# Attention: the output weights split inside the first two tiles, the keys' copy ahead of the sinks, the sinks read as one row

## The reference

```
q = rope(hn @ w_q) * HEAD_DIM**-0.5                    # 16 heads of 64
s = where(band, q @ k.T, -inf)                         # 128 queries x 256 keys of a block
m = max(max(s), sink)                                  # one sink per head
e = exp(s - m)
pr = e / (sum(e) + exp(sink - m))
o = pr @ v                                             # (seq, 1024)
h = h + o @ w_o                                        # w_o is 1024 x 1024
```

## Time and profile before

| | us |
|---|---|
| median of 3 runs | 5109.37 |
| lowest and highest | 5103.85, 5109.4 |
| the profiled execution | 5106.4 |
| its span, first to last instruction | 5104.7 |

### The profile page before, as it was taken

The page is one execution under the profiler, slowest core; times in us unless marked ns, Lnnn a source line. Parts: engine busy times, 40 slices in busy tenths (PEclk is TensorE's granted clock), DMA queues, the critical chain, the costliest instruction groups (busy, mean ns, idle before and its releaser), DMA issues. The chain is left out here.

```text
span 5104.7 us, 90848 instructions
## 1 busy us (share of the span) xinstructions
PE 4660.7 (91%) x29444; PEld 2961.6 (58%) x29509; DVE 2867.1 (56%) x5891; ACT 2022.9 (40%) x2962; POOL 1585.7 (31%) x1163
## 2 busy tenths in 40 slices
PE   7985999999995999999589999986999999997999
PEld 6953677676663444444256666643676667665444
DVE  5774444444444555555378888873445444443676
ACT  5844443343332222222145555534343343331443
POOL 1103443444340111111033333312444444431332
PEclk9987999999997999999799999997999999999999
DMA  7968999998996666666367677757999989985664
GB/s 232 323 225 299 297 323 305 289 322 283 292 287 189 184 186 187 187 185 182 88 160 177 175 179 179 177 179 260 297 314 311 296 295 318 284 275 172 246 233 169
DMA packets 1217386, 1220.13 MB, mean 239 GB/s; under 512 B 880656, under 2 KB 908304, under 8 KB 1217296
## 3 DMA queue, kind: packets, MB, share of 16 engines
q1 hardware_dynamic: 1171216, 1051.21, 68.2%
q0 software_dynamic: 46080, 167.79, 9.4%
HBM read 738.57 MB, written 270.53 MB: 198 GB/s over the span
## 5 line engine op out<-in xcount | busy, mean ns | idle before, releaser
L824 POOL TENSOR_TENSOR ex_w_lo<-ex_raw,ex_w_hi 128x2048 bf16<-128x2048 f32 x192 | 780.4, 4093 | 1154.6 <-ACT ex_w_hi L882 1154.6
L882 ACT ACTIVATE ex_w_hi<-ex_raw 128x2048 bf16<-128x2048 f32 x384 | 707.2, 1900 | 395.4 <-PE ex_ps_y L110 190.7
L986 PE MATMUL ex_ps_gate<-ex_xT,ex_w_hi 128*128 128x0 bf16 x2048 | 569.4, 278 | 160.4 <-DMA ex_xT<-ex_xrow 132.3
L987 PE MATMUL ex_ps_gate<-ex_xT,ex_w_hi 128*128 128x0 bf16 x2048 | 569.2, 278 | 0.0
L988 PE MATMUL ex_ps_gate<-ex_xT,ex_w_lo 128*128 128x0 bf16 x2048 | 568.7, 278 | 0.0
L986 PE MATMUL ex_ps_up<-ex_xT,ex_w_hi 128*128 128x0 bf16 x2048 | 558.4, 273 | 0.0
L987 PE MATMUL ex_ps_up<-ex_xT,ex_w_hi 128*128 128x0 bf16 x2048 | 558.3, 273 | 0.0
L988 PE MATMUL ex_ps_up<-ex_xT,ex_w_lo 128*128 128x0 bf16 x2048 | 558.3, 273 | 0.0
L966 DVE COPY ex_y<-ex_ps_y 128x512 f32 x324 | 224.1, 692 | 567.0 <-PE ex_ps_y L110 522.8
L950 DVE TENSOR_TENSOR ex_aT<-ex_silu,ex_ps_up 128x384 bf16<-128x384 f32 x256 | 141.8, 554 | 708.6 <-PE ex_ps_up L988 525.2
L108 PE MATMUL ex_ps_y<-ex_w_hi,ex_aT 128*128 128x512 bf16 x1296 | 493.0, 380 | 8.1 <-DVE ex_aT L954 7.6
(11 more groups left out here) (345 smaller groups left out, 9693.2 us busy)
## 6 DMA issues: line engine op xcount, KB each, us to landing
ex_raw<-in_w_exp_gate SPq DMA_DIRECT2D x128, 1024.0 KB, 10.9
ex_raw<-in_w_exp_up SPq DMA_DIRECT2D x128, 1024.0 KB, 12.5
ex_raw<-in_w_exp_down SPq DMA_DIRECT2D x128, 1024.0 KB, 7.2
y_rows<-ex_y SPq DMA_DIRECT2D x162, 512.0 KB
up_rows<-rt_up_out SPq DMA_DIRECT2D x64, 512.0 KB, 2.6
cb_hin<-h_mid SPq DMA_DIRECT2D x64, 512.0 KB, 3.5
cb_up_in<-up_rows SPq DMA_DIRECT2D x64, 512.0 KB
mix_x<-in_x SPq DMA_DIRECT2D x32, 512.0 KB, 5.3
```

Source lines behind the costliest of these rows:

```text
L824: eng.tensor_tensor(w_lo[u][:, w], raw[:, c, :], w_hi[u][:, w], ALU.subtract).then_inc(lo_done, 1)
L882: act.activation(w_hi[u][:, c * WCHUNK:(c + 1) * WCHUNK], raw[:, c, :], ACT.Copy).then_inc(hi_done, 1)
L986: pe.matmul(out, hi, x_hi, start=j == 0, stop=False)
L987: pe.matmul(out, hi, x_lo, start=False, stop=False)
```

## The change

The block `split_weights` is gone. Four buffers `raw` belong to attention now, and the split is done among the pairs of the steps 0 and 1: `w_hi(c)` on ACT, `w_lo(c)` on DVE, at the places that `hi_steps` and `lo_steps` give as (step, pair). SP issues the first four chunks' loads (eight DMAs) at the start of step 0, ahead of h3, and the other four chunks one by one ahead of the transposes of pairs 4 to 7 of that step. TensorE waits for the low halves before the projections of step 1.

The sinks are read with one DMA as one row, in the order of the heads, after q_in and kv_in; `head(c, k)` finds the column. DVE writes them into the score tiles behind the first copy of the keys. `g_ffn` and the router's loads stand at the end of step 0 on SP; the waits for them are in step 2. The one wait at the head of DVE and TensorE is gone.

```diff
-        split_weights(nc, C, "aw", [], jobs)
+        raw = [m.sb(f"raw{i}", [P, D]) for i in range(HALF)]
...
+        hi_steps = {(0, 0): 0, (0, 1): 1, (0, 2): 2, (0, 3): 3, (0, 7): 4, (1, 0): 5, (1, 1): 6, (1, 2): 7}
+        lo_steps = {(0, 1): 0, (0, 2): 1, (0, 3): 2, (0, 4): 3, (1, 0): 4, (1, 1): 5, (1, 2): 6, (1, 3): 7}
+        def head(c, k):
+            return NP * (c // HALF) + HALF * k + c % HALF
...
         @block.sync
-                        sp.dma_start(sink[:, 8 * jj + k:8 * jj + 8:2],
-                                     row(A["sinks"][0][8 * jj + 4 * k:8 * jj + 4 * k + 4])).then_inc(loaded, 16)
             sp.dma_start(q_in[0][:], q_t[0]).then_inc(q_ld[0], 16)
             sp.dma_start(kv_in[0][:], kv_t[0]).then_inc(kv_ld[0], 16)
-            sp.dma_start(g_ffn[:], row(A["g_ffn"][1])).then_inc(loaded, 16)
-            load_router(nc, sp, A, w_router, bias, 1, loaded)
+            sp.dma_start(sink[:], row(A["sinks"][0])).then_inc(sink_loaded, 16)
+            def weight(jj, i):
+                wait(sp, w_lo_done, HALF * (jj - 1) + i + 1)
+                for k in (0, 1):
+                    sp.dma_start(raw[i][HEAD * k:HEAD * k + HEAD, :], src[jj, i, k]).then_inc(w_loaded[i], 16)
...
                     sp.dma_start(q_in[u][:], q_t[s + 2]).then_inc(q_ld[u], 16)
+                if isinstance(s, int) and s == 0:
+                    for i in range(HALF):
+                        weight(0, i)
...
                 for c in range(NP):
+                    if isinstance(s, int) and s == 0 and c >= HALF:
+                        weight(1, c - HALF)
                     if cur:
                         turn(s, c)
...
+                if isinstance(s, int) and s == 0:
+                    sp.dma_start(g_ffn[:], row(A["g_ffn"][1])).then_inc(loaded, 16)
+                    load_router(nc, sp, A, w_router, bias, 1, loaded)
...
         @block.scalar
+            def w_hi(c):
+                act.wait_ge(w_loaded[c % HALF], 32 * (c // HALF + 1))
+                act.activation(wo[:, 0, c, :], raw[c % HALF][:], ACT.Copy).then_inc(w_hi_done, 1)
...
+                    if isinstance(s, int) and (s, c) in hi_steps:
+                        w_hi(hi_steps[s, c])
                     if c == 2 and prev:
                         out_hi(s - 1, 1)
...
         @block.vector
-            dve.wait_ge(loaded, 16 * 9)
+            def sinks():
+                dve.wait_ge(sink_loaded, 16)
...
+            def w_lo(c):
+                dve.wait_ge(w_hi_done, c + 1)
+                dve.tensor_tensor(wo[:, 1, c, :], raw[c % HALF][:], wo[:, 0, c, :], ALU.subtract).then_inc(w_lo_done, 1)
...
+                    if isinstance(s, int) and (s, c) in lo_steps:
+                        w_lo(lo_steps[s, c])
                     if c == 1 and prev2:
+                        if isinstance(s, int) and s == 2:
+                            dve.wait_ge(loaded, 16 * 5)
...
                         last.then_inc(kT_done, 1)
+                        if isinstance(s, int) and s == -1:
+                            sinks()
...
         @block.tensor
-            pe.wait_ge(loaded, 16 * 9)
...
                     if c == 0 and prev:
+                        if isinstance(s, int) and s == 1:
+                            pe.wait_ge(w_lo_done, HALF)
...
                     if c == 4 and prev:
+                        if isinstance(s, int) and s == 1:
+                            pe.wait_ge(w_lo_done, NP)
```

More of the change, by code:

```diff
@@ L1018, in _ @@
             chunks(pe, chunk)
[L1021 to L1069, removed]
 class Rotary:
@@ L1769, in attention_phase @@
         src = A["w_o"][0].rearrange("(jj s i e) n -> jj i s e n", jj=2, s=2, i=4)
-        jobs = [([(slice(0, HEAD), src[c // 4, c % 4, 0]), (slice(HEAD, P), src[c // 4, c % 4, 1])], None,
-                 wo[:, 0, c, :], wo[:, 1, c, :]) for c in range(NP)]
-        split_weights(nc, C, "aw", [], jobs)
+        raw = [m.sb(f"raw{i}", [P, D]) for i in range(HALF)]
         g_ffn = m.sb("g_ffn", [P, D])
@@ L1805, in attention_phase @@
         ps_log, ps_k = ps_t[:, 0:NLOG], ps_o[:, 0, 0:2 * P].rearrange("p (j n) -> p j n", j=2)
-        loaded, fixed = m.sems("loaded fixed")
+        sink_loaded, loaded, fixed, w_hi_done, w_lo_done = m.sems("sink_loaded loaded fixed w_hi_done w_lo_done")
+        w_loaded = [m.sem(f"w_loaded{i}") for i in range(HALF)]
         q_ld, kv_ld, h3_ld, h4_st, row_st = ([m.sem(f"{n}{u}") for u in (0, 1)] for n in ("q_ld", "kv_ld", "h3_ld", "h4_st", "row_st"))
@@ L1847, in _ @@
         def _(sp):
-            with nc.allow_non_contiguous_dma(reason="sinks in head-pair order, once"):
-                for jj in (0, 1):
-                    for k in (0, 1):
-                        sp.dma_start(sink[:, 8 * jj + k:8 * jj + 8:2],
-                                     row(A["sinks"][0][8 * jj + 4 * k:8 * jj + 4 * k + 4])).then_inc(loaded, 16)
             sp.dma_start(q_in[0][:], q_t[0]).then_inc(q_ld[0], 16)
             sp.dma_start(kv_in[0][:], kv_t[0]).then_inc(kv_ld[0], 16)
-            sp.dma_start(g_ffn[:], row(A["g_ffn"][1])).then_inc(loaded, 16)
-            load_router(nc, sp, A, w_router, bias, 1, loaded)
+            sp.dma_start(sink[:], row(A["sinks"][0])).then_inc(sink_loaded, 16)
[3 more added lines that the diff above has]
+                    sp.dma_start(raw[i][HEAD * k:HEAD * k + HEAD, :], src[jj, i, k]).then_inc(w_loaded[i], 16)
             def turn(t, c):
@@ L1977, in _ @@
         def _(dve):
-            dve.wait_ge(loaded, 16 * 9)
-            for c in range(NP):
-                dve.tensor_copy(score[c][:, :, W:W + 1], sink[:, 2 * c:2 * c + 2].unsqueeze(2)).then_inc(top_open, 1)
+            def sinks():
+                dve.wait_ge(sink_loaded, 16)
+                for c in range(NP):
+                    dve.tensor_copy(score[c][:, :, W:W + 1],
+                                    sink[:, head(c, 0):head(c, 1) + 1:HALF].unsqueeze(2)).then_inc(top_open, 1)
             def top(t, c):
@@ L1990, in top @@
                     last = dve.tensor_tensor_reduce(out=score[c][:, k, 0:W], in0=ps_s[:, c % 2, k, :], in1=mask[:],
-                                                    scale=1.0, scalar=sink[:, n:n + 1], op0=ALU.add, op1=ALU.max,
+                                                    scale=1.0, scalar=sink[:, head(c, k):head(c, k) + 1], op0=ALU.add, op1=ALU.max,
                                                     accum_out=mx[:, n:n + 1])
@@ L2158, in step @@
                     if c == 7 and prev2:
+                        if isinstance(s, int) and s == 2:
+                            pe.wait_ge(loaded, 16 * 5)
                         pe.wait_ge(hnT_done, s - 1)
```

## The result

The changed kernel takes 5086.1 us (median of 6 runs, 5081.2 to 5090.8) where the kernel before takes 5111.6 (6 runs, 5103.9 to 5123.6): a ratio of 0.9947, interval 0.9937 to 0.9956, or 27 us faster. The forecast was 5078.0 in a range of 5066 to 5088, a gain of 31.4 us. The profiled execution took 5081.2 us, its span is 5079.6. There is one profile of each kernel here.

A forecast was written before the change was run, and what follows sets the result against it. Bound: 53.1 us before attention's first useful work (split block, then scattered sinks holding SP's queue); DVE paces step 0, TensorE later steps. -47.8 + 10.6 + 5.8 = -31.4 us gives 5078.0, range 5066 to 5088.

The forecast's parts named there:

- The start: Attention's head: first transposes 5.3 us after SP's first issue, 47.8 us earlier than before; bounds 44.6 to 48.8.
- Step 0: Split on DVE and ACT: low halves wait for high halves, 10.6 us lost before the keys' copy; bounds 4.6 to 14.
- The second projection's start: Sign in step 1: TensorE's second projection starts 16.4 us later against the first transposes than the 41.5 before.
- Step 1: Split on DVE and ACT, partly absorbed by gaps: low half of the outputs 5.8 us later; ends 1 and 9.
- rival C: TensorE's clock falls to 1.2 GHz after step 1's new gap, slowing the second projection; 3 to 5 us, chance 0.15.
- 5.8 stays: From the second projection of step 1 on, TensorE is the bound, so the 5.8 us delay persists.
- Rival B: DMA queue: loads ahead of the transposes that free POOL's buffers make them 6 to 10 us late; chance 0.2.
- A: The split hides better: without waits for w_hi only DVE's own time counts, 5067 us; chance 0.15.
- D: Four raw buffers move attention's tiles and slow every step; from 1.4 us a step, over 10 us slower; chance 0.03.
- E: Start doesn't come forward: q_in lands late or block code isn't at hand; 3 to 8 us lost, chance 0.07.

The follow-up runs named there:

- sink_row: Kernel before with one edit: sinks read by one DMA as one row in place of four scattered ones, load order kept; ratio 0.9958, 21.5 us faster.
- sinks_third: Changed kernel with the four scattered sink copies back, behind q_in and kv_in; one profile, 870.59 us to the next phase, 17.7 more than the changed kernel.
- warm: Changed kernel plus 26 zero-tile matmuls filling TensorE's gaps in step 1; ratio 0.9931 of the kernel before.
- head_only: Changed kernel with the block split_weights put back, so only attention's head is new; ratio 0.9952 of the kernel before, 24.5 us faster.
- router_early: Changed kernel with g_ffn and the router's loads issued at the end of step -1, not behind step 0; ratio 0.9944 of the kernel before.
- spread: Changed kernel with low halves 0-3 one pair later, high halves 4-7 and their loads earlier; ratio 0.9920 of the kernel before.
- spread_router: Kernel with the spread halves, plus g_ffn and router loads at the end of step -1; 842.22 us to the next phase against 839.43.
- lo_later: Changed kernel with only the four low halves of step 0 moved one pair later; ratio 0.9927 of the kernel before.

## Why the prediction was right, and where it was off

*The start.* Forecast -47.8, measured -48.8. The transposes began 4.3 us after the first issue, the lower end that I had named, not 5.3. The reading of the earlier trace rows (the sinks hold the queue) is shown by sink_row and sinks_third.

*Step 0.* The waits were forecast as 1.2, 2.2, 1.2 and 1.2 us and came as 1.14, 2.16, 1.25 and 1.25, each released by ACT. The step's loss is less than the 10.6: 9.2 to the copy of the keys (28.71 after the transposes, 19.48 before) and 8.4 to the low half of the outputs. DVE waited 1.81 and 0.25 us for the first scores of tile 0, and pair 3's score step came 0.8 us sooner after the transposes than before. TensorE delivered these sooner because its granted clock rose sooner after the transposes. The window from 6.2 to 9.2 us after them, before and in the changed kernel:

```profile
2566.50:2569.50 3.00, 3.00 (x8) 2.25 (x7) 1.81 (x11) 1.66 (x7) 0.45 (x1) 0.50 0.05 18
```

```profile
2513.50:2516.50 3.00, 2.84 (x12) 1.71 (x11) 2.65 (x14) 2.19 (x8) 1.01 (x1) 0.99 0.99 254
```

Here the clock worked in the change's favour, which the sum had not foreseen: luck. It explains the 0.8 us; the rest of what step 0 cost less is not explained. The second projection's start, forecast 16.4 us later against the transposes, came 15.4 later (56.91 against 41.54).

*Step 1.* Forecast 5.8, measured 6.5 to the low half of the outputs. The waits (0.65, 1.25, 2.16, 1.25) are those of the sum, and TensorE's gaps took their part. What was missing is w_lo 7 at 2.02 us and w_lo 4 at 1.54 in place of 1.22: they began while POOL worked. I had weighed this rule of the Trainium skill ("SBUF — State Buffer", section "SBUF: two separate sides": one of DVE and GpSimd holds the shared ports to the end of its instruction) and allowed 1 us; it cost 1.1. I had assumed that POOL's turn would always come first and be over. For w_lo 7 a late DMA undid that; w_lo 4 met an operation of POOL that DVE had released.

*TensorE's clock.* This is the term that I had at zero and as rival C, with 3 to 5 us and a chance of 0.15. It fell, in step 1 and again in step 2: 2.3 us from the low half of the outputs to the statistics of step 2 and 1.6 in step 2, 3.9 in all and within C's price. Rival C is what happened. The step that failed is the sentence that from the second projection on "5.8 stays": it counted the idleness that the edit adds on TensorE as a shift, without asking what the idleness does to the speed of what follows. warm gives 3.4 us of it back; that the 1.6 of step 2 come from the edit's idleness is not sure, since head_only has them without it.

*What else is in the difference.* 0.7 us in step 3 are POOL and DVE in each other's way behind a late transpose, which the sum did not have, and 1.7 in the last step come and go from profile to profile. So 1.0 us better at the start, 2.2 better in step 0, 0.7 worse in step 1, 3.9 worse by the clock, 0.7 worse in step 3 and 1.7 worse in the last step make -27.6 out of -31.4. That the time lies so near the forecast is in part luck: 3.2 us of errors on one side stand against 7.0 on the other.

*The loads.* Rival B, POOL waiting for a transpose behind the router's loads, came true once (5.29 us of idleness), but router_early won back only 0.8 us in step 1 and the 0.7 of step 3. It came in other kernels too: in spread POOL waits 5.93 us in step 1 and from the second low half of the outputs to the statistics of step 2 it takes 16.44 us, where spread_router, with those loads ahead of step 0, takes 15.43, both at a granted clock of 1.00. One us, then; the price of 6 to 10 us was far too high.

*Rivals A, D, E.* A is wrong for this order and right as a hint: spread shows what the split costs once no low half follows its high half. D is out: steps from the fifth on differ by 0.00 us. E did not come.

## What to carry to other kernels

Work moved into an in-order program costs what it takes plus the wait for its producer: keep one slot of the pace-setting engine between an operation and the one on another engine that feeds it (here 12.8 us, nearly half of what the whole change brought). Before a block is taken apart, look for tiny pieces at the head of the queue: one DMA's form was worth 21.5 us, the block itself 3 to 4 with the split placed as in this change. Count a new gap on TensorE twice, as time and as clock. And before a difference of two profiles is put down to an edit, see in which step it arises: 1.7 us in the last step came and went here with no edit near.

## What the runs showed of the hardware

Four DMAs with 512 pieces of 4 bytes each (by the code) held SP's queue for some 19 us at a DMA share of 0.05 (2531.20 to 2550.00, and the earlier trace rows); the same sinks, read as one row by one DMA, took no time that shows (0.35 us of issue in sink_row). The two bulk loads behind them landed 21.7 and 20.2 us after their issue, and SP's own issues stretched from 0.4 to 7.7 us.

A fall of the granted clock outlasts the gap ahead of it. In the changed kernel the gap before the second projection was 3.33 us; TensorE began the second projection at about 2563.6 (its first recorded matmul stands at 2564.04), and its matmuls took 0.63 us (0.38 at full clock) until 2567.9:

```profile
2567.45 0.63 PE L108 MATMUL att_ps_x<-att_wo,att_oT 128*128 128x512 bf16 x1
2567.88 0.54 PE L109 MATMUL att_ps_x<-att_wo,att_oT 128*128 128x512 bf16 x1
2568.25 0.38 PE L110 MATMUL att_ps_x<-att_wo,att_oT 128*128 128x512 bf16 x1
```

A gap of 2.14 us ahead of the first projection of step 2 was followed by half speed once more, where one of 1.74 us before and one of 1.96 in spread were not. But the gap's length does not decide it: one of 1.73 us in head_only, one of 1.74 in lo_later and one of 1.96 in router_early, at the same place, were followed by a fall too. What decides stays open.
